# Mixer attention: next step's scores ahead of the transposes, unnormalised sums token by value, queries and dilated keys and values stored by residue

## The reference

```python
DILATED_GROUPS = ((128, 1), (512, 4), (2048, 16))     # window, dilation
q_a = partial_rope(q_a.reshape(B, S, nh, 128), positions)     # first 32 channels turn
k_a = partial_rope(k_a.reshape(B, S, nh, 128), positions)
for g, (window, dilation) in enumerate(DILATED_GROUPS):
    o, lse = dilated_window_attention(q_a[:, :, g], k_a[:, :, g], v_a[:, :, g], window, dilation)
    outs.append(o); lses.append(lse)
alpha = jax.nn.softmax(jnp.stack(lses, axis=0), axis=0)
att = jnp.sum(alpha[..., None] * jnp.stack(outs, axis=0), axis=0)
```

## Time and profile before

| what | value |
|---|---|
| median of 3 runs | 2696.98 us (2696.88 to 2697.7) |
| the profiled execution's own time | 2698.24 us |
| its span | 2696.2 us |
| PE busy | 2547.0 us, 94% of the span |
| DVE, ACT, POOL busy | 38%, 36%, 39% |
| mean granted PE clock | 0.968 of full |

### The profile page before, as it was taken

How to read it: one execution, slowest core, us unless ns; L and a number is a source line. 1 busy time by engine, 2 the same in 40 slices (tenths; PEclk the granted TensorE clock), 3 DMA queues, 4 the chain that set the end, 5 groups by cost and what they waited for, 6 DMA issues and landing times.

```text
span 2696.2 us, 39906 instructions
## 1 busy us (share of the span) xinstructions
PE 2547.0 (94%) x14064; PEld 2034.3 (75%) x14064; DVE 1037.7 (38%) x1883; ACT 966.1 (36%) x1375; POOL 1050.9 (39%) x756
## 2 busy tenths in 40 slices
PE   8899989999999999999999899998999999899997
PEld 6766657886878888788887577676777777688885
DVE  2145567564555542322211533343222344422213
ACT  3133343213366652344422322123343342444421
POOL 3111123002545555455555533432333345555554
PEclk9699999999999999999999899999999999899998
DMA  4101112002323333233333211221222222233332
GB/s 166 32 32 31 39 47 63 3 3 71 95 85 100 94 101 101 95 100 93 97 104 103 82 61 58 79 63 48 71 70 75 66 82 89 64 99 94 101 101 86
DMA packets 56734, 205.09 MB, mean 76 GB/s; under 512 B 6828, under 2 KB 7596, under 8 KB 56268
## 3 DMA queue, kind: packets, MB, share of 16 engines
q1 hardware_dynamic: 55152, 196.45, 23.5%
q10 hardware_dynamic: 1504, 7.49, 0.8%
HBM read 201.81 MB, written 2.10 MB: 76 GB/s over the span
## 4 chain that ended last, share of the span: by engine, by line
PE 86%; DVE 7%; ACT 4%; issue 2%; DMA 0%; DVEq 0%; POOL 0%; ACTq 0%; SPq 0%
PE psum L348 84%; ACT blocks L1024 1%; DVE blocks L1436 1%; DVE ml_qk L1901 1%; PE psum L498 1%; ACT w_hi L960 0%; PE psum L860 0%; DVE zm L1482 0%; DVE psum L1358 0%; ACT s_cmp L1024 0%; PE psum L550 0%; PE psum L500 0%; DVE soft L1442 0%; DVE blocks L1455 0%; DVE blocks L1454 0%
## 5 line engine op out<-in xcount | busy, mean ns | idle before, releaser
L321 POOL TENSOR_TENSOR w_lo<-raw,w_hi 128x512 fp32r<-128x512 f32 x732 | 1020.4, 1414 | 1614.5 <-ACT w_hi L960 1614.3
L348 PE MATMUL psum<-h_hi,w_hi 128*128 128x512 f32 x2192 | 895.6, 409 | 57.2 <-DVE h_lo L1364 26.7
L348 PE MATMUL psum<-h_lo,w_hi 128*128 128x512 f32 x2192 | 868.0, 396 | 0.0
L960 ACT ACTIVATE w_hi<-raw 128x1024 fp32r<-128x1024 f32 x366 | 385.8, 1055 | 799.8 <-PE psum L348 782.2
L348 PEld LDWEIGHTS psum<-h_hi,w_hi 128*128 128x128 f32 x2192 | 420.3, 192 | 187.5 <-issue 85.5
L348 PE MATMUL psum<-h_hi,w_lo 128*128 128x512 f32 x2192 | 549.5, 390 | 0.0
L348 PEld LDWEIGHTS psum<-h_lo,w_hi 128*128 128x128 f32 x2192 | 420.3, 192 | 91.0 <-issue 7.4
L348 PEld LDWEIGHTS psum<-h_hi,w_lo 128*128 128x128 f32 x2192 | 412.5, 188 | 87.7 <-issue 1.4
L1342 DVE TENSOR_TENSOR tmp<-psum,rst 128x512 f32<-128x512 f32 x108 | 74.7, 691 | 369.9 <-PE psum L348 369.4
L348 PE MATMUL psum<-hid_hi,w_hi 128*128 128x512 f32 x528 | 208.7, 395 | 0.0
L348 PE MATMUL psum<-hid_lo,w_hi 128*128 128x512 f32 x528 | 208.5, 395 | 0.0
(11 more groups left out here) (367 smaller groups left out, 2769.9 us busy)
## 6 DMA issues: line engine op xcount, KB each, us to landing
raw<-in_w SPq DMA_DIRECT2D x366, 512.0 KB, 3.6
x<-in_x SPq DMA_DIRECT2D x4, 512.0 KB, 6.5
tmp<-in_cmp_w ACTq DMA_DIRECT2D x1, 2048.0 KB, 7.3
x<-in_x ACTq DMA_DIRECT2D x1, 2048.0 KB, 7.8
out_y<-x SPq DMA_DIRECT2D x8, 256.0 KB, 2.1
mask<-in_mask ACTq DMA_DIRECT2D x1, 1536.0 KB
masks<-in_masks ACTq DMA_DIRECT2D x1, 768.0 KB, 9.3
lora<-in_lora ACTq DMA_DIRECT2D x1, 512.0 KB, 5.2
```

The source lines that it names most:

```text
L321: pool.tensor_tensor(w_lo[:, g.slot, part], raw[:, g.slot, part], w_hi[:, g.slot, part].bitcast(F32), ALU.subtract).then_inc(sem("lo_ready ...
L348: return pe.matmul(out, lhsT, rhs, start=start, stop=stop)
L960: act.activation(w_hi[:, g.slot], raw[:, g.slot], ACT.Copy).then_inc(sem("hi_ready"), 1)
```

## The change

- PE: the scores of step r+1 (`att_scores(r + 1)`) are made at the start of step r; those of step 0 between units 7 and 8. The half unit of a step is cut in two quarters, and the transposes (`att_turn`) lie between them. The sums `att_pv(r)` end their own step instead of following the next step's scores.
- The probabilities are not divided. The sums are token by value: the transposed probabilities are stationary, the values move, and `v_tm` has a 129th column of ones, so that the last column of the product is the softmax's sum. DVE divides the 128 x 128 result (`att_norm`), PE transposes it back into `p2` (`att_back`), and DVE writes the output from there (`att_output`).
- The exponential no longer accumulates. `att_p` and its small columns have two buffers.
- Queries, and the keys and values of groups 1 and 2, are written sorted by residue when they leave PSUM, so that matmuls and transposes read them without a stride. DVE reads the bank, the norm factors and the rotation tables with a step of four elements instead. Unit 3 (keys of group 0) and unit 6 (its values) stay in token order.
- On ACT, `v_take(0)` and `att_exp(0)` stand after the `high_part` of unit 9 instead of that of unit 10.

```diff
         def v_blocks / v_take
-  src = tmp[:, 4 + n, tok(b)] if n == 0 else tmp[:, 4 + n, b::4]
-  last = pe.transpose(p3[:, tok(b)], src, ident[:])
+  last = pe.transpose(p3[:, tok(b)], tmp[:, 4 + n, tok(b)], ident[:])
+                    def att_scores(r):
+                        if r:
+                            pe.wait_ge(sem("att_nb"), 4 * hh + r)
+                        else:
+                            pe.wait_ge(sem("roped"), 6 * hh + 6)
+                        mm(p4, qk_st[:, 0, tok(r)], qk_st[:, 3])
+                        for n in (1, 2):
+                            last = mm(p5[:, tok(n - 1)], qk_st[:, n, tok(r)], qk_st[:, 3 + n, tok(r)])
+                        last.then_inc(sem("att_scores"), 1)
+                    def att_turn(r):
+                        pe.wait_ge(sem("att_exp"), 4 * hh + r + 1)
+                        pe.wait_ge(sem("att_pt_a"), 4 * hh + r)
+                        pe.wait_ge(sem("att_pt_b"), 4 * hh + r)
+                        for n in range(6):
+                            last = pe.transpose(..., att_p[:, r % 2, tok(n)], ident[:])
+                        last.then_inc(sem("att_tm"), 1)
+                    def att_pv(r):
+                        pe.wait_ge(sem("att_pt_a"), 4 * hh + r + 1)
+                        pe.wait_ge(sem("att_pt_b"), 4 * hh + r + 1)
+                        pe.wait_ge(sem("att_normed"), 4 * hh + r)
+                        for n in range(6):
+                            v = v_tm[:, 0, n] if n < 4 else v_tm[:, n - 3, r]
+                            last = mm(p3[:, 0:129], att_pT[:, tok(n)], v, n == 0, n == 5)
+                        last.then_inc(sem("att_pv"), 1)
+                    def att_back(r):
+                        pe.wait_ge(sem("att_normed"), 4 * hh + r + 1)
+                        pe.wait_ge(sem("att_out"), 4 * hh + r)
+                        pe.transpose(p2[:, 0:128], att_on[:], ident[:]).then_inc(sem("att_back"), 1)
                     for c in range(1, 9):
                         unit(gu + c, ou + c, h_hi, h_lo)
                         ...
+                        if c == 7:
+                            att_scores(0)
                     v_blocks(2)
...
+                    for r in range(4):
+                        c, k = 9 + r // 2, 4 * (r % 2)
+                        if r < 3:
+                            att_scores(r + 1)
+                        unit(gu + c, ou + c, h_hi, h_lo, ks=range(k, k + 2))
+                        att_turn(r)
+                        unit(gu + c, ou + c, h_hi, h_lo, ks=range(k + 2, k + 4))
+                        if r:
+                            att_back(r - 1)
+                        if r == 0:
+                            pe.wait_ge(sem("v_tm_ready"), 3 * hh + 3)
+                        att_pv(r)
                     unit(gu + 11, ou + 11, h_hi, h_lo)
-                    att_pv(3)
+                    att_back(3)
```

On ACT:

```diff
                     for c in range(9):
                         high_part(gu + c)
-                        if c == 8:
+                        if c == 7:
                             v_take(0)
+                            att_exp(0)
                     v_take(1)
                     v_take(2)
                     for r in range(4):
-                        act.wait_ge(sem("att_nb"), 4 * hh + r + 1)
-                        act.activation(att_p[:], att_p[:], ACT.Exp, ..., accum_out=att_small[:, 4:5])
+                        if r < 3:
+                            att_exp(r + 1)
                         act.wait_ge(sem("att_tm"), 4 * hh + r + 1)
+                        act.wait_ge(sem("att_pv"), 4 * hh + r)
                         act.activation(att_pT[:, 0:512], p6, ACT.Copy).then_inc(sem("att_pt_a"), 1)
                         if r % 2:
                             high_part(gu + 9 + r // 2)
```

On DVE (`att_max` is the old masked maximum with its bias, into buffer r % 2; `by_residue` is the view "p (m r) -> p r m"):

```diff
                     for c in range(9):
-                        take(gu + c, ou + c, qk_st[:, c] if c < 6 else tmp[:, c - 2])
+                        dst = qk_st[:, c] if c < 6 else tmp[:, c - 2]
+                        if c in (3, 6):
+                            take(gu + c, ou + c, dst)
+                        else:
+                            ...
+                            dve.tensor_tensor(dst.rearrange("p (r m) -> p r m", r=4), by_residue(psum[:, o.slot]),
+                                              by_residue(rst[:]), ALU.mult).then_inc(sem(f"freed{o.slot}"), 1)
                         ...
+                        if c == 7:
+                            att_max(0)
                     for r in range(4):
...
+                        if r < 3:
+                            att_max(r + 1)
+                        dve.wait_ge(sem("att_tm"), 4 * hh + r + 1)
+                        dve.wait_ge(sem("att_pv"), 4 * hh + r)
                         dve.tensor_copy(att_pT[:, 512:768], p7[:, 0:256]).then_inc(sem("att_pt_b"), 1)
                         if r % 2:
                             c = 9 + r // 2
                             take(gu + c, ou + c, tile_of(gates, 2 * hh + r // 2))
+                        if r:
+                            att_output(r - 1)
+                        att_norm(r)
                     att_output(3)
```

More of the change, by code:

```diff
@@ L211, in build_program @@
         qk_st = sb("qk_st", [128, 6, T], scope=att)
-        v_tm = sb("v_tm", [128, 3, TB, 128], scope=att)
+        v_tm = sb("v_tm", [128, 3, TB, 129], scope=att)
         rope = sb("rope", [32, 2, T], scope=att)
@@ L216, in build_program @@
         mask2 = sb("mask2", [128, 4, 768], scope=att)
-        att_p = sb("att_p", [128, 768], scope=att)
+        att_p = sb("att_p", [128, 2, 768], scope=att)
+        att_on = sb("att_on", [128, 128], scope=att)
         att_pT = sb("att_pT", [128, 768], scope=att)
-        att_small = sb("att_small", [128, 8], scope=att)
+        att_small = sb("att_small", [128, 2, 4], scope=att)
+        att_rcp = sb("att_rcp", [128, 1], scope=att)
         att.close()
@@ L812, in rotate @@
                             pe.wait_ge(sem("consts2_in"), 96)
+                        if c == 0:
+                            pe.wait_ge(sem("att_out"), 4 * hh)
                         slot = (161 + 11 * q + c) % 2
@@ L825, in v_blocks @@
                         for b in range(TB):
-                            src = tmp[:, 4 + n, tok(b)] if n == 0 else tmp[:, 4 + n, b::4]
-                            last = pe.transpose(p3[:, tok(b)], src, ident[:])
+                            last = pe.transpose(p3[:, tok(b)], tmp[:, 4 + n, tok(b)], ident[:])
                         last.then_inc(sem("v_tm_done"), 1)
+                    def att_scores(r):
[12 more added lines that the diff above has]
+                        for n in range(6):
+                            last = pe.transpose((p6[:, tok(n)] if n < 4 else p7[:, tok(n - 4)]),
+                                                att_p[:, r % 2, tok(n)], ident[:])
+                        last.then_inc(sem("att_tm"), 1)
[11 more added lines that the diff above has]
+                        pe.transpose(p2[:, 0:128], att_on[:], ident[:]).then_inc(sem("att_back"), 1)
                     for c in range(1, 9):
@@ L1234, in v_take, with att_exp @@
                         act.wait_ge(sem("v_tm_done"), 3 * hh + n + 1)
-                        act.activation(v_tm[:, n].rearrange("p b d -> p (b d)"), p3, ACT.Copy)\
+                        act.activation(v_tm[:, n, :, 0:128], p3.rearrange("p (b d) -> p b d", b=TB), ACT.Copy)\
                             .then_inc(sem("v_tm_ready"), 1)
+                    def att_exp(r):
+                        act.wait_ge(sem("att_nb"), 4 * hh + r + 1)
+                        act.activation(att_p[:, r % 2], att_p[:, r % 2], ACT.Exp, bias=att_small[:, r % 2, 3:4],
+                                       scale=128 ** -0.5).then_inc(sem("att_exp"), 1)
                     for c in range(9):
                         high_part(gu + c)
-                        if c == 8:
+                        if c == 7:
                             v_take(0)
+                            att_exp(0)
                     v_take(1)
@@ L1809, in _, with by_residue @@
             rms_rstd(4)
+            dve.memset(v_tm[:, :, :, 128:129], 1.0)
+            def by_residue(a):
+                return a.rearrange("p (m r) -> p r m", r=4)
             with dve.Fori(0, 2) as i:
@@ L1818, in rope_it @@
                         dve.wait_ge(sem(f"freed{(ou + c).slot}"), (ou + c).half() + 1)
-                        dve.tensor_tensor(qk_st[0:32, c], qk_st[0:32, c], rope[:, 0], ALU.mult)
-                        dve.tensor_tensor(rope_t[:], p2[0:32], rope[:, 1], ALU.mult).then_inc(sem("rope_a"), 1)
+                        x1, x2 = qk_st[0:32, c], p2[0:32]
+                        cos, sin, t = rope[:, 0], rope[:, 1], rope_t[:]
+                        if c != 3:
+                            x1, x2, t = (a.rearrange("p (r m) -> p r m", r=4) for a in (x1, x2, t))
+                            cos, sin = by_residue(cos), by_residue(sin)
```

(27 more changed lines are left out.)

41 lines of the change are left out of this document (2 added, 39 removed).

## The result

The changed kernel takes 2670.85 us (median of 5 runs, 2665.97 to 2678.11) against 2697.65 us before (2696.88 to 2699.09): ratio 0.9906, 95% interval [0.9887, 0.9924]. The profiled execution took 2670.85 us with a span of 2668.8 us. The kernel is faster, as forecast, but by more: 2679.6 us was forecast, with a range from 2674 to 2690 us.

What follows compares the result with a forecast made beforehand. PE was taken as the bound, with its waits. Per head 3.65 + 2.63 - 0.52 - 0.4 = 5.36, four heads 21.4, less 0.6 and 3.4: 17.4 us, so 2679.6 us; range 2674 to 2690.

Steps and rivals of the forecast that it cites:

- The stretch after unit 8: Unit 8's end to step 1's transposes' end, per head: 6.88 us in place of 11.87; third block's transposes after 1.60.
- The exponentials and the copies: ACT's work in attention steps: hidden behind PE, the copy of transposed blocks covered by 0.1 us only.
- the stepped DVE operations: Takes and rotations reading with a step of four: 1.46 us each, covered up to 1.81, so costing nothing.
- the start of the next stage: It hangs on the last output, then a load; that output moves with PE's end, so the gain is passed on.
- The transposes back: One added PE transpose (`att_back`) in each step: 4 x 0.13 = 0.52 us per head.
- the rivals: Four: clock low as today, 0.12; ACT bounds steps, 0.13; DVE bounds units 0 to 5, 0.04; steps still wait, 0.06.
- The scores without a stride: Each attention step's scores on PE: 0.43 us less, 1.34 in place of 1.77.
- The clock: PE's low clock after unit 8: falls in one head in two at 1.7 us, 3.4 us lost; bounds 0 and 13.4.
- a fall in every head: If transposes don't count as PE being busy, the clock falls in all heads: 6.8 us, 2683.0 us in total.
- The seams: Two more PE seams a step, the cut unit and the single transpose: 0.05 us taken, 0.4 per head.
- The waits ahead of the sums: PE waiting for ACT's copy before the sums: 0.05 us in three steps of each head, 0.6 us in all.
- The range's lower end: Whole kernel with no clock loss and no seams: 2679.6 - 3.4 - 1.6 - 0.6, 2674 us.

Runs made afterwards that it cites:

- the divided kernel: Changed kernel with probabilities divided on DVE as before, sums value by token, no column of ones or transpose back: 2667.2 us, ratio to before 0.9895.
- the run in token order: Changed kernel with queries, keys and values stored in token order again, so scores and value transposes read every fourth column: 2681.23 us, ratio to before 0.9943.
- The cut alone: Kernel before with each half unit issued as two calls, nothing between them: 2695.61 us, ratio to before 0.9996.
- the two later sets: Changed kernel measured again twice, unedited, beside the kernel before: 2674.48 and 2674.54 us, ratios 0.992 and 0.9913.

## Why the prediction was right or wrong

What held. PE's path through the attention was the bound. The stretch after unit 8 came out as worked: 1.59 us for 1.60, about 6.9 for 6.88. The exponentials and the copies are hidden, the stepped DVE operations too, at 1.07 to 1.15 us where 1.46 was taken, and the start of the next stage moved along. The transposes back cost PE some 2.1 us in all by the divided kernel (4.17 less 2.11 at the stop), forecast 2.1. None of the rivals came.

What was wrong is four terms of the sum, all to the same side. The forecast's 17.4 us and the measured 25.65 of the stretch differ by 8.3:

- The scores without a stride, "I take 0.43". This is the step of the prediction that failed, as the range had nothing for it. By the run in token order it is 0.60 a step, 2.7 us more in sixteen steps. The prediction read a step's parts between starts of weight loads and called the groups behind the scores "the same work". They are not: a part of the stepped passes' time falls on the group behind, 1.46 us for the sums before against 1.34 after, and 1.40 for the quarter unit in the token order run against 1.27. The durations in the earlier trace rows had offered 0.52, and the prediction took less, in case only three of the four small passes show it. All four do, and the two passes of 512 columns, left out there, are longer too.
- The clock, "one head in two at 1.7: 3.4 us". It fell in no head of three profiles: off by 3.4 us, the largest error in size. The prediction had put 1.42 us busy in 3.4 us of the next stage beside a gap of 2.1 to 2.5 us, and called that near the edge. Around the wait PE was in fact busy for 2.20 us in 3.4, with the transposes on either side of it. The Trainium skill (TensorE: Matmul & The Clock Gate, Part 4: PE-mode transpose) says that transposes do not count as PE being busy, and from this the prediction worked out a fall in every head. No head fell; whether they count is not shown by that.
- The seams, "I take 0.05, 0.4 per head". The cut alone costs nothing: 1.6 us.
- The waits ahead of the sums, "0.6 us in all". There is none, as ACT starts its copy 0.09 us before the exponential's recorded end and the copy has 0.46 us to spare: 0.6 us.

Together 8.3. That it comes out to a tenth is partly luck: the 0.4 us of the token order run that no row explains and the next stage's stop, 10.15 us for 9.87, are left out and nearly cancel.

The range's lower end took back the clock, the seams and the waits in full, 5.6 us, and came to 2674.0. With the scores' 2.7 us it would have been 2671.3, and 2670.85 was measured; the rest is within what executions differ by. Luck has a part in the miss too: in the two later sets the same kernel had medians of 2674.48 and 2674.54 us, inside the range. The range held no term for the time ahead of the mixer, because the three times of the kernel before lay within 0.8 us; its later times go from 2692.34 to 2702.61 us.

In parts, from the runs: the storing gives 10 us (367.42 less 357.45), the new order with the softmax's new form 15.7 (383.10 less 367.42). The second part is made up, by an estimate, of 7.2 us of recorded waits (12.0 less 4.8) and of the low clock, some 20 us at half speed before and none after, which is up to 10 us of work; the transposes back take off 2.1. How it divides between waits and clock is not measured more closely. With the next step's scores ahead, the division has a whole step to hide in, so in this order unnormalised sums give nothing and cost a transpose a step. What they would give in the old order was not run.

## What to carry to other kernels

Moving work ahead of its need can make other tricks superfluous: after a reordering, test again what was added against the old wait, here the unnormalised sums with their transpose back. When a group of matmuls is priced by starts of weight loads, look also at the group behind it. Store once in the order in which the bound engine reads, on an engine that has time. Where several blocks go through one bank, put independent work between them before counting their copies as unavoidable.

## What the runs showed of the hardware

Passes of 128 columns over operands with a step of four floats last 405 to 407 ns on PE, 274 in sequence. The six such passes of a step's scores (four of 128 columns, two of 512) cost 0.60 us a step, of which the starts of their own weight loads show 0.46. DVE reads PSUM and the norm factors with a step of four floats at 1.15 us for 128 x 512, against 0.69 in sequence. ACT's copy began 0.09 us before the recorded end of the exponential ahead of it. The same kernel, in two executions, was granted 0.94 and 0.91 over the same 540 us.
